# One core, a two-layer diffusion backbone: merge and output projection in one block, gate stores in another queue, an earlier load of the keys, 16-bit one-hots and four late row buffers

## What is computed

```python
for l in range(2):
    u = modulate(rms_norm(x), shift, scale)
    p = u @ w_in                       # queries, keys, values, gates of three branches
    # retention, conformer and hyena branches: b_ret, b_conf, b_hy
    x = x + gate * ((sig(p_r) * b_ret + sig(p_c) * b_conf + sig(p_h) * b_hy) @ w_out)
    h = modulate(rms_norm(x), shift2, scale2)
    q = h @ peer_wq                    # 8 heads, two halves each
    s = q . sub_keys                   # 2 x 128 scores per head and token
    # top 16 of each half, top 16 of their sums, softmax gates: 128 experts of 16384 per token
    out = sum_k gelu(peer_u[e_k] . h) * gate_k * peer_v[e_k]
    x = x + gate2 * out
```

## Time and profile before

| | |
|---|---|
| median of the three runs | 5533.78 us |
| the profiled execution | 5530.9 us |
| its span in the profile | 5529.1 us |
| TensorE busy | 4768.5 us (86%) |
| VectorE busy | 4286.6 us (78%) |
| ScalarE busy | 1807.0 us (33%) |
| GpSimd busy | 994.0 us (18%) |
| mean granted TensorE clock | 0.928 |
| DMA, mean | 223 GB/s |

### The profile page before, as it was taken

One profiled execution on the slowest core, in us unless ns is written; L12 is line 12 of the kernel. 1 busy time (PEld: TensorE's weight loads), 2 busy tenths in 40 slices (PEclk: granted clock), 3 DMA queues, 4 the chain that ended last, 5 costly groups with the idle time before them and its releaser, 6 DMA issues. The chain is left out here.

```text
span 5529.1 us, 68759 instructions
## 1 busy us (share of the span) xinstructions
PE 4768.5 (86%) x23090; PEld 3760.6 (68%) x23090; DVE 4286.6 (78%) x7460; ACT 1807.0 (33%) x3293; POOL 994.0 (18%) x714
## 2 busy tenths in 40 slices
PE   7887849898996669999999889889896659999998
PEld 3776728535764448888888648744674548888886
DVE  5466588677547879999999868768635989999997
ACT  2232321221233643333333321221122744444443
POOL 0000017300000003333333216400000002222221
PEclk9988969999997879999999989999998769999999
DMA  6432329602123569999999839612121259999996
GB/s 224 177 112 86 126 92 371 209 31 76 62 72 106 167 204 382 393 397 385 388 392 393 316 115 342 242 43 69 61 85 53 75 153 374 381 383 371 377 373 246
DMA packets 458293, 1230.39 MB, mean 223 GB/s; under 512 B 210227, under 2 KB 244308, under 8 KB 396950
## 3 DMA queue, kind: packets, MB, share of 16 engines
q1 hardware_dynamic: 355896, 613.96, 32.2%
q0 software_dynamic: 102240, 614.51, 28.2%
HBM read 1168.78 MB, written 59.51 MB: 222 GB/s over the span
## 5 line engine op out<-in xcount | busy, mean ns | idle before, releaser
L2630 POOL DMA_INDIRECT arena<-in_peer_uv,kept x448 | 638.3, 1425 | 3347.6 <-POOLq L2481 1944.7
L236 PE MATMUL psum<-v_ring_hi,w_parts 128*128 128x512 f32 x2560 | 837.2, 392 | 9.6 <-DVE v_lo L2736 9.6
L236 PE MATMUL psum<-h_hi,u_ring_hi 128*128 128x384 f32 (+1 forms) x2048 | 671.3, 328 | 35.1 <-DVE u_lo L2731 34.8
L236 PE MATMUL psum<-h_hi,u_lo 128*128 128x384 f32 (+1 forms) x2048 | 665.1, 325 | 0.0
L236 PE MATMUL psum<-h_lo,u_ring_hi 128*128 128x384 f32 (+1 forms) x2048 | 664.1, 324 | 0.0
L2771 DVE SCALAR_TENSOR_TENSOR arena<-arena 128x1024 f32<-128x1024 f32 x448 | 558.5, 1282 | 19.2
L2761 DVE CUSTOM_DVE_ANT_0 arena<-arena 128x1024 f32<-128x1024 f32 x448 | 536.1, 1219 | 35.3 <-DMA arena<-in_peer_uv,kept 34.3
L236 PEld LDWEIGHTS psum<-v_ring_hi,w_parts 128*128 128x128 f32 x2560 | 482.0, 188 | 106.4 <-DVE v_lo L2736 11.3
L236 PE MATMUL psum<-v_lo,w_parts 128*128 128x512 f32 x1280 | 502.3, 392 | 0.0
L236 PEld LDWEIGHTS psum<-h_hi,u_ring_hi 128*128 128x128 f32 x2048 | 386.1, 189 | 78.4 <-DVE u_lo L2731 37.5
L236 PEld LDWEIGHTS psum<-h_lo,u_ring_hi 128*128 128x128 f32 x2048 | 386.4, 189 | 5.6 <-issue 0.5
(11 more groups left out here) (393 smaller groups left out, 9597.5 us busy)
## 6 DMA issues: line engine op xcount, KB each, us to landing
kept<-in_mix SPq DMA_DIRECT2D x312, 512.0 KB, 3.5
kept<-in_peer_u SPq DMA_DIRECT2D x256, 512.0 KB, 6.7
kept<-in_peer_uv SPq DMA_DIRECT2D x256, 512.0 KB, 5.7
kept<-in_ada SPq DMA_DIRECT2D x96, 512.0 KB, 4.3
gate_scratch<-arena SPq DMA_DIRECT2D x11, 4096.0 KB, 21.1
arena<-gate_scratch SPq DMA_DIRECT2D x64, 384.0 KB, 5.7
arena<-gate_scratch SPq DMA_DIRECT2D x64, 320.0 KB, 8.7
spec_scratch<-arena POOLq DMA_DIRECT2D x4, 2048.0 KB, 10.6
```

The source lines that it names most:

```text
L236: done = pe.matmul(out, lhs[x], rhs[y], start=first and j == 0, stop=last and j == 2)
L2630: pool.indirect_dma_start(rows[q % NBUF], None, peer_uv, bass.IndirectOffsetOnAxis(ap=at, axis=0))\
```

## The change

1. Merge and output projection become one block of the program. u is handed over chunk by chunk, behind block 0 of the weights; each merged chunk is rounded (ScalarE) and split (VectorE) in the course of the merge; TensorE begins output blocks 0 and 1 with the chunks that are there and adds the last chunk behind them. Both `pe_again` calls of the pair are gone. `bank_free` is raised after the two multiplications.
2. The keys are loaded at the start of the query block, ahead of its weights, in SP's list.
3. The gate stores are issued by ScalarE, after chunk 17 and at the end of a tile, and no longer by SP.
4. The one-hots of side i are compared in 16 bit for every chunk, those of side j in 16 bit for each third chunk (ScalarE then copies them to f32) and in f32 as half an instruction for the others.
5. In "dots" 22 late rows in place of 24, sixteen of them over four buffers (two of the ring's are added), the last six over two; two more rows are taken beside the value blocks; the edges of `hp` are cleared row by row.

```diff
-        LATE_ROWS = {"dots": 24, "adds": 32}
+        LATE_ROWS = {"dots": 22, "adds": 32}
+        WIDE = 16
-        late_bufs = {"dots": [area(M0 + 18552 + 1024 * k, D) for k in range(2)],
+        late_bufs = {"dots": [area(M0 + 18552 + 1024 * k, D) for k in range(2)] + ring_bufs[4:6],
...
-                back = 6 if q < late else len(late_bufs[kind])
+                back = 6 if q < late else 2 if kind == "dots" and q - late >= WIDE + 2 else 4
                 if q - back >= (FIRST_ROWS if q < late else late):
                     pool.wait_ge(ctx_free.sem, ctx_free.at(q - back + 1))
+                elif kind == "dots" and q == late + 2:
+                    pool.wait_ge(ctx_free.sem, ctx_free.at(late))
...
-            deal = {"dots": [1, 2, 3, 3, 3, 2, 3, 3] + [5, 5, 5, 5, 4, 4, 4, 3] + [3, 3, 3, 3, 3, 2, 3, 3] + 8 * [3] + 12 * [2],
+            deal = {"dots": [1, 2, 3, 3, 3, 2, 3, 3] + [5, 5, 5, 5, 5, 4, 4, 4] + [3, 3, 3, 3, 3, 2, 3, 3] + 8 * [3]
+                    + [3, 2, 3, 2, 3, 2, 3] + [1, 1, 1, 1, 0],
...
-        def stage_merge_others(s, m):
+        def stage_merge_out(s, m):
+            OUT = 24
+            mo_hi, mo_lo = m["merged_split"]
...
-                    load_ahead(sp, 24)
+                    load_ahead(sp, OUT + 8)
...
                             for j in range(len(x[0])):
+                                if n == 0:
+                                    pe.wait_ge(u_chunk_split.sem, u_chunk_split.at(j + 1))
...
-                    pe_again(pe, 7, 8 if s == "X" else 5)
-                    pe.wait_ge(dve_a.sem, dve_a.at(1))
...
+                    pe.wait_ge(bank_free.sem, bank_free.at(4 + 21))
+                    for k in range(2):
+                        pe.wait_ge(block_lo.sem, block_lo.at(OUT + k + 1))
+                        for kc in range(KC - 1):
+                            pe.wait_ge(merged_split.sem, merged_split.at(kc + 1))
+                            out_product(k, kc)
+                    pe.wait_ge(merged_split.sem, merged_split.at(KC))
+                    for k in range(2):
+                        out_product(k, KC - 1).then_inc(blocks_done.sem, 1)
+                    for k in range(2, 8):
+                        pe_split_block(pe, hi2, OUT, OUT, 4 * (k // 4), k % 4, (mo_hi, mo_lo), T)
...
-                    act_round(act, m["u"], u_hi)
                     act_round_block(act, hi2, 0, 0, 0)
+                    for kc in range(KC):
+                        act.activation(u_hi[:, kc, :], m["u"][:, kc, :], ACT.Copy).then_inc(chunk_rounded.sem, 1)
+                    act_round_block(act, hi2, 0, 0, 1)
...
                             gate(i, n)
+                            if n % 3 == 1 and 4 * i + n // 3 > 0:
+                                round_merged(4 * i + n // 3 - 1)
+                    act_round_block(act, hi2, OUT, 0, 1)
+                    round_merged(7)
+                    for k in range(2, 8):
+                        act_round_block(act, hi2, OUT, 0, k)
...
+                    dve_rest_block(dve, hi2, OUT, 1)
+                    rest_merged(7)
+                    for k in range(8):
+                        add_out(k)
+                        if k + 2 < 8:
+                            dve_rest_block(dve, hi2, OUT, k + 2)
...
+        def stage_query(s, split, evacuate, l):
...
+                    sp.dma_start(keys_sb.rearrange("p a b -> p (a b)"), keys[l]).then_inc(keys_in.sem, 16)
                     load_ahead(sp, 8)
...
+            def both_16(n):
+
+                return n % 3 == 0
...
+                        if both_16(n):
+                            act.activation(hot_j[n % 3], hots_16[n % 3][:, 1].rearrange("p n t -> p t n"), ACT.Copy)
                         for q in range(4):
                             at = 4 * n + q
-                            x = hot_i[n % 3][:, q, :]
-                            last = act.activation(x, x, ACT.Copy, scale=weight[:, at:at + 1])
+                            last = act.activation(hot_i[n % 3][:, q, :], hots_16[n % 3][:, 0, :, q], ACT.Copy, scale=weight[:, at:at + 1])
...
+                            if k == 17:
+                                store(n - 1, 0)
...
+                        store(n - 1, chunks_of(n - 1) // 16 - 1)
...
-                            dve.tensor_tensor(hot[n % 3], iota4, picked_t[:, 0:2, at].unsqueeze(3).broadcast_to([P, 2, 4, NK]),
-                                              ALU.is_equal).then_inc(equal_ready.sem, 1)
+                            at, parts = slice(4 * n, 4 * n + 4), 2 if both_16(n) else 1
+                            last = dve.tensor_tensor(hots_16[n % 3][:, 0:parts], iota_16.unsqueeze(1).broadcast_to([P, parts, NK, 4]),
+                                                     picked_16[:, 0:parts, at].unsqueeze(2).broadcast_to([P, parts, NK, 4]), ALU.is_equal)
+                            if not both_16(n):
+                                last = dve.tensor_tensor(hot_j[n % 3], iota4, picked_t[:, 1, at].unsqueeze(2).broadcast_to([P, 4, NK]),
+                                                         ALU.is_equal)
+                            last.then_inc(equal_ready.sem, 1)
```

More of the change, by code:

```diff
@@ L370, in counted_ctx @@
                 ctx_rows_in[k].add(16 * len(range(k, late - FIRST_ROWS, 6)))
-            for k in range(len(late_bufs[kind])):
-                late_rows_in[k].add(16 * len(range(k, P - late, len(late_bufs[kind]))))
+            for k in range(4):
+                uses = [n for n in range(P - late) if n % (2 if kind == "dots" and n >= WIDE else 4) == k]
+                late_rows_in[k].add(16 * len(uses))
             ctx_free.add(P)
@@ L1201, in blocks_with_rows @@
                             else:
+                                if beside == "dots":
+                                    dve.drain()
+                                    edges(m["hp"][:, j - 32:j - 31, :], 1)
                                 keep_hp(j // 4 - 8, n)
@@ L1214, in blocks_with_rows @@
                                 dve.drain()
+                            if j == 31 and beside == "adds":
                                 edges(m["hp"], 1)
@@ L1965, in _ @@
+                    dve_rest_block(dve, hi2, 0, 0)
+                    for kc in range(KC):
+                        dve.wait_ge(chunk_rounded.sem, chunk_rounded.at(kc + 1))
+                        dve.tensor_tensor(u_lo[:, kc, :], m["u"][:, kc, :], u_hi[:, kc, :].bitcast(F32), ALU.subtract).then_inc(u_chunk_split.sem, 1)
+                    dve_rest_block(dve, hi2, 0, 1)
+                    dve_rest(dve, m["hc"], hc_hi, hc_lo, 0)
+                    dve_rest(dve, z, z_hi, z_lo, 4)
                     for i in range(2):
```

122 lines of the change are left out of this document (60 added, 62 removed).

## The result

The changed kernel takes 5414.38 us, median of four runs (5406.16 to 5428.7), where the kernel before takes 5533.0 beside it: ratio 0.9779, 95% interval 0.9763 to 0.9795. Measured once more beside it, it took 5407.81 against 5539.66: 0.9766 (0.9752 to 0.9779). Forecast were 5399 and a range of 5365 to 5450. The profiled execution has a span of 5412.7 us, 116.4 shorter than before.

What follows compares the result with a forecast made beforehand. TensorE bounds X's merge, VectorE is fullest in the choice of experts; idle stretches of the bound engine were counted. 29 + 27 + 27 + 38 + 14 = 135 us off 5530.9 gives 5396, median 5399 us; range 5365 to 5450.

Steps and rivals of the forecast that it cites:

- term 29: Merge and output in one block: saves 29 us, 12.3 in X twice and 4.6 in C; bounds 18 and 34.
- C's 4.6: Merge and output in C: 5.7 us gained at the exit, 0.9 at the entry, 2 lost to rounding.
- The term for the clock: Entry of X's merge: a 3.4 us stretch at 1.2 GHz falls on real products, costing 1.7 us.
- the new wait at block 2: X's output: block 2 can be rounded and split only from block 0's end, a new TensorE wait of 2.0 us.
- both long waits stand beside a change of TensorE's clock: Entry and exit of X's merge before the change: slow clock near both; 1558 to 1570 has mean granted clock 0.86.
- term 27: Two parts, 27 us each: TensorE's waits for keys, with slower scores; loads held at issue behind layer 0's gate stores.
- Rival (a): Gate stores: stores and loads collide on the same 16 engines, VectorE keeps its 30.1 us wait; 5426 us, chance 0.1.
- Rival (d): Gate stores: ScalarE's own sequencer is held by each store, eleven stores cost 212 us; 5611 us, chance 0.03.
- term 38: 16-bit one-hots in the choice of experts: 9.1 us a tile off VectorE, 38 us in all; bounds -8 and 46.
- VectorE's interval was 2.5 and becomes 2.2: it stays the bound: One-hots, first two tiles: VectorE's interval stays above ScalarE's 1.9, so 9.1 us a tile is saved.
- ScalarE takes over in the third tile: Layer 0's packed third tile: VectorE's interval would fall from 1.97 to 1.65, ScalarE becomes the bound, saving lost.
- term 14: Four late row buffers beside the projection: 21 us of TensorE waits go, 2.3 and 5 come back; bounds 7 and 19.

Runs made afterwards that it cites:

- `e_warm`: The changed kernel with products of constants again ahead of the merge's first product, 4 in X and 3 in C; 5412.78 us, ratio to before 0.9755.

## Why the prediction was right, and where its terms were off

The median stands 15 us above the forecast in the first measurement, 9 in the second, and inside the range; against the kernel before beside it the gain is 119 and 132 us, where 135 were forecast. The five undone parts add up to 31 + 21 + 27 + 25 + 13 = 117 us (rows as the mean of their last two pairs; with the first, which gave 0, it would be 113) of the 126 that the mean ratio gives. Each term carries some 10 us of noise, so the sum shows no large overlap between the parts, and not more than that. That the second measurement comes so near is luck in part: the one-hots gave 11 us less than forecast, the merge 4 more, and layer 0's experts, which the forecast left alone, were 4.7 us shorter than in the kernel before. The prediction calls the experts over half of the span; they are 2.1 of the 5.5 ms.

- **Merge and output** (term 29): 33. C's 4.6 measured 4.2. X was put at 12.3 a layer; 13.4 and 12.8 from trace to trace, 14.6 and 14.5 in the undone part. The term for the clock was right at the entry (3.4 us at 0.5, half of it lost) and the new wait at block 2 was 1.78 for 2.0, with no clock lost in the changed kernel. The reading behind it was wrong in one point: "both long waits stand beside a change of TensorE's clock". In the kernel before only the exit does, in the second line; at the entry, behind 1.88 us of idle, the clock stays at 1.00:

```profile
1417.00:1421.00 4.00, 4.00 (x10) 1.85 (x11) 3.45 (x6) 4.00 (x8) 0.00 (x0) 1.00 0.02 4
...
1560.00:1564.00 4.00, 3.19 (x4) 1.51 (x5) 3.04 (x6) 3.21 (x7) 0.00 (x0) 0.59 0.13 52
```

  The undone kernel's exit was a little longer than that of before, with 10.84 us of constants instead of 9.62, which is most of the 1.2 and 1.7 between the two accounts.
- **Keys** (term 27): 20 in the undone part, 25 from trace to trace. What was off is C: 4.8 of wait and 1.7 of clock, less 1 to 2 for late ring loads, 5 in all. The wait for the ring was 3.7 us in two traces, 2.0 to 2.3 in six and under 1 in two, and C's query stage, 42.1 to 46.2 us in these ten, was on average 2.3 us shorter than the 46.4 of before; the scores behind it are 1.5 shorter. With the keys moved to the norm, away from the ring loads, the stage takes 40.3 and 41.2 us. In X layer 0's wait was 9.0 us before and 6.5 in the undone part.
- **Stores** (term 27): 28.3 in layer 0, 0.5 in layer 1. Rival (a) said that the queue makes no difference; the 19.33 us at the issue were the stall. Rival (d) fell: ScalarE's issue of a store took 0.43 us, and nothing on it stood behind one.
- **One-hots** (term 38): 27. This is the step that failed, in size and in layer 0. The 9.1 us a tile of VectorE's time were right (9.2), the durations near (0.681 for 0.63, the pair 1.10 for 0.99 with overlap). Wrong was "VectorE's interval was 2.5 and becomes 2.2: it stays the bound" for layer 0: there half of the saving became small waits for free buffers (4.0 and 5.5 us of 9.2 reached the tile), while layer 1, which has no conditioning on TensorE and ScalarE beside the gates, kept 8.3. That the conditioning is the reason is argued from this difference; no run took it out. That ScalarE takes over in the third tile was right, but I put its cost at zero; its copies make the tile 0.8 to 2.8 us longer than with 32 bits, and the three tiles some 4.5 us longer than with side j of the third tile in 32 bits alone.
- **Rows** (term 14): 13.3, of it 8.6 behind the last block, where 8 were forecast, and 4.3 in waits for block rests, where 13.6 less 2.3 and 5, so 6.3, were. One wait of 3.36 us is left there, at 1032 us.
- **What the forecast did not have**: the experts. They do the same work in 1111.7 to 1130.9 us, and the stage of the rows varies by 5 us between executions of the same order. The 12 us that looked lost behind the choice lie within that: the second execution of the same kernel has the experts at 1111.7.

## What to carry to other kernels

A transfer can be held at its issue by what stands ahead of it in its list, as the load behind the 4 MB store was for 19.33 us: look at the length of the issue itself, and either cut the large transfer or give it another list. Less busy time on the fullest engine was worth nearly its full amount in layer 1 (8.3 of 9.2 us a tile) and half in layer 0; in the tile that was already packed, work shifted to the helper made it slower. And before a loss in untouched code is explained, the same kernel should be profiled twice.

## What the runs showed of the hardware that I had not expected

- The hold at the issue grows with the store ahead: 19.33 us behind 4 MB in 256-byte pieces, 5.22 behind 1 MB.
- Constants in a gap can prevent the slow clock and not only absorb it: at the merge's entry in X 3.4 us at 0.5 followed 4.96 us of idle TensorE, and none followed 1.87 us of idle with constants behind it. At the exit in the kernel before the idle time ahead of the constants was 3.25 us, and the slow stretch came and fell on them (0.59 from 1560 to 1564). The Trainium skill, "TensorE: Matmul & The Clock Gate", section "Why this matters for your kernels", advises no gap above about 3 us. The rows agree on the long gaps, but staying under it was not always enough: after the wait of 1.78 us at block 2 the clock stayed at 1.00 in the changed kernel and fell to 0.5 for 3.4 us in layer 1 of `e_warm`.
- A copy of 512 elements from 16 bit to f32 with its two inner dimensions swapped takes ScalarE 669 ns, where an eviction of 512 f32 takes 589 ns; a weighing of 128 16-bit elements read at a stride takes 404 ns, where one of 128 f32 side by side took 392.
- The same experts' stage, 1083 to 1089 us of TensorE's busy time, varies by 19 us between executions, at 378 to 385 GB/s.
